# One-hot weights of the second token block shared out three ways, and 24 retrieved rows added during that stage

## The reference, cut to what matters

```
expert, gate = product-key top-k(h)            # 128 experts for each token
act = gelu(einsum('td,ted->te', h, u_table[expert]))
out = einsum('te,ted->td', gate * act, v_table[expert])
x = LayerNorm(alpha * x + (1 + gate2) * out) * ln2_g + ln2_b
```

## Time and profile before

| what | value |
| --- | --- |
| median of 3 runs | 2711.09 us (2710.27 to 2713.92) |
| the profiled execution | 2719.48 us |
| its span | 2717.0 us |
| PE busy | 2374.5 us, 87% |
| DVE busy | 2061.6 us, 76% |
| ACT busy | 1009.8 us, 37% |
| POOL busy | 869.9 us, 32% |

### The profile page before, as it was taken

One profiled execution on the slowest core, in us unless ns is written; L12 is line 12 of the kernel. 1 busy time (PEld: TensorE's weight loads), 2 busy tenths in 40 slices (PEclk: granted clock), 3 DMA queues, 4 the chain that ended last, 5 costly groups with the idle time before them and its releaser, 6 DMA issues.

```text
span 2717.0 us, 34317 instructions
## 1 busy us (share of the span) xinstructions
PE 2374.5 (87%) x12532; PEld 1891.1 (70%) x12532; DVE 2061.6 (76%) x2517; ACT 1009.8 (37%) x1428; POOL 869.9 (32%) x733
## 2 busy tenths in 40 slices
PE   4799999999999999999969867666666699999996
PEld 3688877888888887888859857656656664444442
DVE  7777779788888786554576999999999786665577
ACT  2254543344444444433343322227776750000000
POOL 0000011222222221000001566656666454444344
PEclk9799999999999999999989988887787799999998
DMA  9767669566666565555746899999999879999997
GB/s 385 292 215 243 226 228 358 208 213 215 217 217 215 207 215 193 207 189 186 258 178 230 353 419 419 419 419 388 404 407 388 344 256 414 413 413 414 414 413 277
DMA packets 144867, 819.86 MB, mean 302 GB/s; under 512 B 16680, under 2 KB 19360, under 8 KB 70480
## 3 DMA queue, kind: packets, MB, share of 16 engines
q0 software_dynamic: 93200, 477.21, 44.7%
q1 hardware_dynamic: 48480, 335.95, 33.3%
q10 hardware_dynamic: 3040, 4.68, 0.5%
HBM read 813.55 MB, written 4.23 MB: 301 GB/s over the span
## 4 chain that ended last, share of the span: by engine, by line
PE 61%; DVE 23%; DMA 7%; issue 5%; ACT 3%; POOL 1%; ACTq 0%; DVEq 0%; POOLq 0%
PE aux L1155 16%; DVE rrow L2151 9%; PE ps L706 8%; PE ps L707 8%; PE ps L712 7%; PE ps L731 4%; PE ps L732 4%; PE ps L737 4%; DMA rrow<-in_peer_u,acc 3%; DVE acc L1668 2%; DVE rrow_first L2151 1%; DVE wlo L1619 1%; PE aux L992 1%; DMA dskip<-in_D_skip 1%; DMA vden<-in_p_vd 1%
## 5 line engine op out<-in xcount | busy, mean ns | idle before, releaser
L1619 DVE TENSOR_TENSOR wlo<-raw,whi 128x2048 fp32r<-128x2048 f32 x216 | 499.6, 2314 | 292.4 <-ACT whi L1174 281.8
L1174 ACT ACTIVATE whi<-raw 128x2048 fp32r<-128x2048 f32 x216 | 412.1, 1910 | 664.1 <-PE ps L712 386.8
L2236 DVE SCALAR_TENSOR_TENSOR ps<-vrow,acc,ps 128x1024 f32<-128x1024 f32 x231 | 297.5, 1288 | 177.2 <-DMA vrow<-in_p_vg,acc 162.1
L2414 POOL DMA_INDIRECT rrow<-in_peer_u,acc x219 | 354.1, 1617 | 220.3 <-DVE dots L2151 115.2
L2151 DVE CUSTOM_DVE_ANT_0 rrow<-rrow,h 128x2048 f32<-128x2048 f32 x172 | 385.1, 2288 | 16.8 <-DMA rrow<-in_peer_u,acc 16.3
L2414 POOL DMA_INDIRECT vrow<-in_p_vg,acc x256 | 247.4, 966 | 265.3 <-DVE ps L2236 178.0
L2328 POOL DMA_DIRECT2D ada_in<-in_p_ada x128 | 69.3, 542 | 673.2 <-DVEq L1775 529.2
L1096 PE MATMUL aux<-hT,rT 128*128 128x128 f32 x1792 | 233.8, 294 | 37.1 <-ACT rT L1503 37.1
L731 PE MATMUL ps<-h_hi,whi 128*128 128x256 f32 x1040 | 264.6, 295 | 0.0
L1096 PEld LDWEIGHTS aux<-hT,rT 128*128 128x128 f32 x1792 | 226.7, 209 | 46.0 <-issue 31.7
L706 PE MATMUL ps<-whi,h_hi 128*128 128x512 f32 x576 | 235.1, 408 | 24.7 <-ACT whi L1174 24.1
(11 more groups left out here) (361 smaller groups left out, 4337.7 us busy)
## 6 DMA issues: line engine op xcount, KB each, us to landing
raw<-in_p_in SPq DMA_DIRECT2D x104, 1024.0 KB, 4.9
ada_in<-in_p_ada POOLq DMA_DIRECT2D x128, 512.0 KB, 4.8
vden<-in_p_vd SPq DMA_DIRECT2D x64, 1024.0 KB, 8.0
ada_in<-in_p_ada SPq DMA_DIRECT2D x32, 1024.0 KB, 10.1
raw<-in_p_so SPq DMA_DIRECT2D x32, 1024.0 KB, 4.7
raw<-in_p_mo SPq DMA_DIRECT2D x16, 1024.0 KB, 7.2
raw<-in_p_bc SPq DMA_DIRECT2D x16, 1024.0 KB, 6.4
raw<-in_p_mix SPq DMA_DIRECT2D x16, 1024.0 KB, 4.8
```

Source lines behind the costliest of these rows:

```text
L1174: F(whi[:, n % 2, :, 0:cols_], raw[:, n % 4, :, 0:cols_], ACT.Copy).then_inc(hi_ready, 1)
L1619: V.tensor_tensor(wlo[:, n % 2, :, 0:cols_], raw[:, n % 4, :, 0:cols_], whi[:, n % 2, :, 0:cols_].bitcast(F32), ALU.subtract).then_inc(lo_ ...
L2236: last = V.scalar_tensor_tensor(o, row, w, o, ALU.mult, ALU.add)
L2414: return G.indirect_dma_start(out=dst, out_offset=None, in_=table, in_offset=bass.IndirectOffsetOnAxis(ap=eid_all[:, r:r + 1], axis=0))
```

## The change

The three kinds of groups are laid out in a pattern of eight: three WEIGHED (as before: VectorE compares both tiles, ScalarE multiplies), four ALL_DVE (VectorE compares the first tile, and makes the second in four fused compare-and-multiply instructions of 128 columns) and one ALL_ACT (ScalarE makes both by squares, then 1 - x clipped at zero, then the multiplication, as the first block's groups are made; the squares are issued one and two groups ahead). In the weights stage 24 rows are added instead of 8: TensorE adds the even rows 0 to 22, after groups 1, 4 and 7 of each eight, and VectorE the odd rows 1 to 23, after groups 0, 3 and 6, into the idle bank pair 1. After the stage VectorE copies pair 1 to SBUF and adds it to pair 0, and only then may SP load `vden` units 2 and 3 (the copy lies in their memory). VectorE then goes on from row 24 instead of row 8. The diff, cut:

```
+        def made(n):
+            return (WEIGHED, ALL_DVE, WEIGHED, ALL_DVE, ALL_DVE, ALL_ACT, WEIGHED, ALL_DVE)[n % 8]
...
-        FIRST_PE, TAIL_PE = OHB // 4, range(225, BLK * SEL, 2)
+        FIRST, TAIL_PE = 24, range(225, BLK * SEL, 2)
+        FIRST_PE = range(0, FIRST, 2)
...
                         sp_.wait_ge(wt_done, BLK * OHB)
+                        sp_.wait_ge(merged, merged_before + 1)
...
                     weights_of(1, n)
-                    if n % 4 == 3:
-                        pe_add(n // 4, n // 4 == 0, n // 4 == FIRST_PE - 1)
+                    if n % 8 in (1, 4, 7):
+                        r = FIRST_PE[n // 8 * 3 + (1, 4, 7).index(n % 8)]
+                        pe_add(r, r == FIRST_PE[0], r == FIRST_PE[-1])
...
+                def squares(n, half):
+                    act.wait_ge(wt_done, OHB + n - 3)
+                    for t in range(2 * half, 2 * half + 2):
+                        for k in range(2):
+                            last = F(oh[1][:, n % 4, k, t, :], niota, ACT.Square, scale=-1.0,
+                                     bias=selT[:, k, n * OHT + t:n * OHT + t + 1])
...
+                def hots(n):
...
+                    F(flat, flat, ACT.Relu, scale=-1.0, bias=con[:, C_ONE:C_ONE + 1]).then_inc(act_step, 1)
+                    act.wait_ge(act_step, done)
...
                 for n in range(OHB):
-                    if by_act(n):
+                    for half in range(2):
+                        if n + 2 - half < OHB and made(n + 2 - half) == ALL_ACT:
+                            squares(n + 2 - half, half)
+                    if made(n) == ALL_ACT:
+                        hots(n)
+                    if made(n) != ALL_DVE:
                         weigh(n)
...
-                    o = ps[:, r // SEL, :, :].rearrange("p a n -> p (a n)")
+                    o = ps[:, 1 if r < FIRST else r // SEL, :, :].rearrange("p a n -> p (a n)")
...
+                    elif made(n) == ALL_DVE:
+                        V.tensor_tensor(o[:, 0], niota.unsqueeze(1).broadcast_to([P, OHT, P]),
+                                        selT[:, 0, t4].unsqueeze(2).broadcast_to([P, OHT, P]), ALU.is_equal)
+                        for t in range(OHT):
+                            token = n * OHT + t
+                            last = V.tensor_scalar(o[:, 1, t, :], niota, selT[:, 1, token:token + 1],
+                                                   selT[:, 2, token:token + 1], ALU.is_equal, ALU.mult)
+                        last.then_inc(oh_ready, 1)
+                    if n % 8 in (0, 3, 6):
+                        add_row(2 * (n // 8 * 3 + n % 8 // 3) + 1)
+                dve.wait_ge(vrow_pe_used, scores_all + len(FIRST_PE))
+                dve.wait_ge(vrow_used, adds_by(False, FIRST - 1))
+                dve.wait_ge(wt_done, BLK * OHB)
+                both = [ps[:, k, :, :].rearrange("p a n -> p (a n)") for k in range(2)]
+                link(V.tensor_copy(on_dve[:, :], both[1]))
+                link(V.tensor_tensor(both[0], both[0], on_dve[:, :], ALU.add))
+                dve.sem_inc(merged, 1)
...
-                for r in range(FIRST_PE, BLK * SEL):
+                for r in range(FIRST, BLK * SEL):
...
-                    if r < FIRST_PE:
+                    if r in FIRST_PE:
                         weight_diagonal(r)
```

More of the change, by code:

```diff
@@ L327, in build, with steps_made @@
         oh = [at(f"oh{b}", o * KB, [P, OHN[b], 2, OHT, P]) for b, o in enumerate((150, 62))]
[L329 to L335, removed]
+        WEIGHED, ALL_DVE, ALL_ACT = range(3)
+        def made(n):
+            return (WEIGHED, ALL_DVE, WEIGHED, ALL_DVE, ALL_DVE, ALL_ACT, WEIGHED, ALL_DVE)[n % 8]
+        def steps_made(kinds, n):
+            return sum(made(k) in kinds for k in range(n + 1))
         QA = KEYS // 2
@@ L360, in build @@
         DV, NVU = D // 2, KEYS // 2
+        on_dve = at("on_dve", 62 * KB, [P, DV])
         vrow = at("vrow", 14 * KB, [P, ROWS, D - DV])
@@ L370, in build @@
         vden = at("vden", 46 * KB, [P, 4, 2, DV])
-        FIRST_PE, TAIL_PE = OHB // 4, range(225, BLK * SEL, 2)
-        adds_on_pe = list(range(FIRST_PE)) + list(TAIL_PE)
+        FIRST, TAIL_PE = 24, range(225, BLK * SEL, 2)
+        FIRST_PE = range(0, FIRST, 2)
+        adds_on_pe = list(FIRST_PE) + list(TAIL_PE)
         late = BLK * SEL - 64
@@ L542, in build @@
         block0_read, block0_before = c_ready, 1
+        act_step, act_before = sumsq_ready, 4
+        merged, merged_before = neg_a, 1
         held = sem("held")
@@ L1108, in weights_of @@
                     m, k = b * OHB + n, n % OHN[b]
-                    if b and by_act(n):
-                        pe.wait_ge(hot_done, OHB + steps_by(True, n))
+                    if b and made(n) != ALL_DVE:
+                        pe.wait_ge(hot_done, OHB + steps_made((WEIGHED, ALL_ACT), n))
                     else:
-                        pe.wait_ge(oh_ready, OHB + steps_by(False, n) if b else n + 1)
+                        pe.wait_ge(oh_ready, OHB + steps_made((ALL_DVE,), n) if b else n + 1)
                     before = m - OHN[b] if n >= OHN[b] else OHB - 1 if b else -1
@@ L1524, in weights_out @@
                     last.then_inc(wt_read, 1)
+                def squares(n, half):
[4 more added lines that the diff above has]
+                                     bias=selT[:, k, n * OHT + t:n * OHT + t + 1])
+                    if half:
+                        last.then_inc(act_step, 1)
+                def hots(n):
+                    done = act_before + 2 * steps_made((ALL_ACT,), n)
+                    act.wait_ge(act_step, done - 1)
+                    flat = oh[1][:, n % 4].rearrange("p k t i -> p (k t i)")
+                    F(flat, flat, ACT.Relu, scale=-1.0, bias=con[:, C_ONE:C_ONE + 1]).then_inc(act_step, 1)
+                    act.wait_ge(act_step, done)
                 def weigh(n):
-                    act.wait_ge(square_done, OHB + steps_by(True, n))
+                    if made(n) == WEIGHED:
+                        act.wait_ge(square_done, OHB + steps_made((WEIGHED,), n))
                     for t in range(OHT):
@@ L1597, in tail_diagonal @@
                     n = adds_by(True, r) - 1
-                    act.wait_ge(vrow_pe_used, scores_all + max(FIRST_PE, n - 3))
+                    act.wait_ge(vrow_pe_used, scores_all + max(len(FIRST_PE), n - 3))
                     F(diag[n % 4], ident, ACT.Copy, scale=w_all[:, r:r + 1]).then_inc(diag_ready, 1)
@@ L2224, in add_row @@
                 def add_row(r):
-                    o = ps[:, r // SEL, :, :].rearrange("p a n -> p (a n)")
+                    o = ps[:, 1 if r < FIRST else r // SEL, :, :].rearrange("p a n -> p (a n)")
                     row, w = vrow[:, vrow_slot(r), :], w_all[:, r:r + 1]
                     dve.wait_ge(vrow_full[r % ROWS], vrow_before[r % ROWS] + 16 * (r // ROWS + 1))
-                    if r % SEL == 0:
+                    if r in (1, SEL):
                         last = V.tensor_scalar(o, row, w, None, ALU.mult)
                     else:
[L2232 to L2235, removed]
+                        dve.wait_ge(vrow_used, adds_by(False, r - 1))
                         last = V.scalar_tensor_tensor(o, row, w, o, ALU.mult, ALU.add)
@@ L2243, in _ @@
                 for n in range(OHB):
-                    if n >= 4:
-                        dve.wait_ge(wt_done, OHB + n - 3)
                     o = oh[1][:, n % 4]
                     t4 = slice(n * OHT, n * OHT + OHT)
[L2248 to L2255, removed]
+                    if n >= 4 and made(n) != ALL_ACT:
+                        dve.wait_ge(wt_done, OHB + n - 3)
@@ new lines, in _ @@
+                    if made(n) == WEIGHED:
+                        V.tensor_tensor(o, niota.unsqueeze(1).unsqueeze(1).broadcast_to([P, 2, OHT, P]),
+                                        selT[:, 0:2, t4].unsqueeze(3).broadcast_to([P, 2, OHT, P]), ALU.is_equal)\
+                            .then_inc(square_done, 1)
+                    elif made(n) == ALL_DVE:
[6 more added lines that the diff above has]
+                        last.then_inc(oh_ready, 1)
```

## The result

The changed kernel took 2722.88 us (median of 13 runs, 2718.07 to 2728.29), the kernel before, run with it, 2715.82 (13 runs). The ratio is 1.0029, with a 95% interval of 1.0020 to 1.0037: 7.9 us slower (the two medians alone differ by 7.1). On the median that the forecast started from, that is 2719.0, against 2720.8.

The account below looks back on a forecast made before the run. TensorE's own matmul pace was taken as the bound: start of the dense stage + 447.5 + 56.4 us. Weights stage +9.7, merge, dense stage and tail 0, sum +9.7 on 2711.09: 2720.8 us, range 2707 to 2729.

Parts of the forecast that it names:

- Weights stage, +9.7: Stage before the dense matmuls: grows from 49.4 to 59.1 us, VectorE's sum 52.1; bounds +2.3 to +17.
- The high end of my bounds: Spacing of a fused instruction on VectorE in the weights stage: 0.15 to 0.283 us, 0.2 taken.
- Entry, exit and coupling: Weights stage beyond VectorE's sum: 5.0 us entry and exit, plus 2 us (0 to 4) for waits between engines.
- GpSimd and the rows at nothing: Weights stage: four more diagonals and 16 more gathers on GpSimd cost nothing, as it works up to eight rows ahead.
- the first rival: Weights stage: supply of rows binds, dense stage starts at 2230, +17 us, 2728; chance 0.12.
- Merge at nothing: Between weights and dense stages: VectorE's 2.6 us merge and the later load of units 2 and 3 cost 0 (0 to 6).
- The second rival: Start of dense stage: units 2 and 3 come late behind the merge, +9.7 and up to 6 us, 2727; chance 0.06.
- Dense stage at nothing: Dense stage: 8.4 MB fewer to gather gains TensorE 0, at most the whole 8.0 us.
- GpSimd's wait of some 39 us: End of dense stage: row 232 issued some 32 us earlier, GpSimd waiting some 39 us instead of 6.88 for row 225.
- Tail unchanged: After the dense stage: the wait for row 225 and the 23 gathers behind it stay the same, 0.
- The last two rivals: Dense stage: relief returns 8.0 us where DMA holds TensorE (0.17); DMA sets dense stage and tail, 2700.5 (0.10).
- the third rival: Dense stage: relief pays where DMA holds TensorE, 8.0 us come back, 2713, or 2706 at the stage's floor; chance 0.17.

Follow-up runs that it names:

- after_tail: Changed kernel with TensorE's share of the last rows beginning at row 241 instead of 225; 0.9975 of the kernel before.
- rows_only: Changed kernel with the old split of groups, keeping the 24 rows and the merge; 1.0046 of the kernel before, +12.5 us.
- before_tail: Kernel before with TensorE's share of the last rows beginning at row 241 instead of 225; 0.9996, not told from no change.
- fused_only: Kernel before with the fused form in VectorE's own eleven groups only; single execution, time not compared, weights stage 48.8 us.
- skip64: Kernel before with the gathers of rows 16 to 79 (33.6 MB) replaced by tiny loads; 0.9992, not told from no change.
- skip16: Kernel before with the gathers of rows 16 to 31 (8.4 MB) replaced by tiny loads; 0.9991, not told from no change.
- split_only: Changed kernel with the three-way split of groups but only the old eight rows, all on TensorE; 1.0032 of the kernel before, +8.7 us.

## Why the prediction was right, and where it was not

The path was right: the time is TensorE's string, and its +8.1 us are the +9.9 of the weights stage, less 2.7 in the dense stage, plus 0.9 in the tail. That 2719.0 came so near to 2720.8 is partly luck, since two errors cancel inside the +9.9, and the other two parts had been put at nothing.

**Weights stage, +9.7: +9.9.** Right in sum, with two errors that cancel. VectorE has 54.9 us of work without a gap, not 52.1: the 64 fused instructions take 17.3 us (54.9 less 12 compares at 1.14, 16 at 0.60 and 12 additions at 1.19), 0.27 each where I took 0.2; that is +4.5, and additions and compares at their spacing give 1.7 back. The high end of my bounds, 0.283, was near. Entry, exit and coupling came to 59.25 - 54.9 = 4.3, not 5.0 + 2: with VectorE plainly the bound, no coupling shows. In the split alone, where ScalarE binds, it does.

**GpSimd and the rows at nothing: right.** Gathers took 1343 ns on average in the groups above, against 937 in the dense stage. The Trainium skill (GPSIMD Engine Reference, Key points) says that GpSimd shares its SBUF interfaces with VectorE and contends with its instructions that have two SBUF inputs or run in a two-port mode. The two means agree with that, but no run here isolates this cause. In the kernel before's stage its eleven gathers took 1495 ns on average, so the change didn't make them slower; no addition waited for a gather, and the first rival falls.

**Merge at nothing: right.** It ends at 2220.31, and the first 672 dense matmuls run through in 288.41 us, the same as before. The second rival falls.

**Dense stage at nothing: -2.7.** The stall is shorter in after than in before. TensorE's timeline of after:

```profile
2529.99 3.29 PE L1163 MATMUL aux<-vden,wt0b 128*128 128x512 f32 x4 [3.21 <-DMA vden<-in_p_vd]
2533.08 2.31 PE L1163 MATMUL aux<-vden,wt 128*128 128x512 f32 x4
2535.23 1.02 PE L1163 MATMUL aux<-vden,wt0b 128*128 128x512 f32 x2
```

And of before:

```profile
2526.86 3.78 PE L1155 MATMUL aux<-vden,wt0b 128*128 128x512 f32 x4 [4.59 <-DMA vden<-in_p_vd]
2530.44 3.11 PE L1155 MATMUL aux<-vden,wt 128*128 128x512 f32 x4
2533.39 1.88 PE L1155 MATMUL aux<-vden,wt0b 128*128 128x512 f32 x4
```

Of the 2.7, 1.4 are the wait and 1.3 the eight matmuls behind it (5.24 us to the next start after, 6.53 before, 3.44 undisturbed). It isn't the relief by itself: with 8.4 or 33.6 MB less and the old weights stage the dense stage took 447.0 and 447.2. The wait goes with the added rows and their merge: 3.2 to 3.4 us in after, after_tail and rows_only (dense stage 444.6 to 444.7), 4.5 to 4.7 in the six kernels without them that keep the stall. Of those six, before_tail and fused_only have a dense stage of 445.9 and 445.8 by losing less behind the wait. Why it is shorter with them stays open. TensorE stalls 309 us into the stage, not 282 as I wrote, which is where the 5 MB are issued; nothing hung on that.

**GpSimd's wait of some 39 us: 20.5.** This step failed in size. I took 16 rows at 2.03 us, the mean over the whole stage, and the rows at its two ends are not at the mean. GpSimd's timeline at rows 31 and 224 of before, then of after (rows 15 and 232 of before stand in the earlier trace rows):

```profile
2239.09 0.94 POOL L2414 DMA_INDIRECT vrow<-in_p_vg,acc  x1 [0.46 <-issue]
2644.16 0.94 POOL L2414 DMA_INDIRECT vrow<-in_p_vg,acc  x1 [0.66 <-issue]
```

```profile
2219.84 0.94 POOL L2457 DMA_INDIRECT vrow<-in_p_vg,acc  x1 [0.30 <-issue]
2626.88 0.94 POOL L2457 DMA_INDIRECT vrow<-in_p_vg,acc  x1 [0.46 <-issue]
```

Before, rows 15 to 31 took 25.0 us, 1.56 each, so at row 31 the lead against the start of the dense stage is 23.8 us (26.0 less 2.2), not 32. At row 224 it is 21.8. The last eight rows take 11.1 us before, 1.39 each, and 16.6 after, and so take 5.5 more of it. Row 232 was issued 425.9 us into the dense stage, before 442.2: 16.3 us earlier, of which the shorter dense stage takes 2.7 and the rest is the added wait (20.51 - 6.88 = 13.6). Bytes over the full rate, 20.3 us, stood in the same paragraph and was nearer. Since the wait was idle time either way (41.3 us of it in skip64 didn't change the time), the total didn't suffer.

**Tail unchanged: +0.9.** Row 233 is gathered 2.7 us after the end of the dense stage in both. In skip16, skip64 and split_only, whose tails nothing touched, the tail took 56.3 to 56.7, and in rows_only, with the added rows, 56.5. The chain shows where the 0.9 lies, in the landing of row 254 (before, then after), behind which both kernels take 17.1 us to the end:

```profile
2693.06 6.85 DMA vrow<-in_p_vg,acc
2694.66 8.03 DMA vrow<-in_p_vg,acc
```

That is 1.2 us more for one gather, which was issued 0.2 earlier after the dense stage. One trace of each doesn't tell whether that belongs to the change; in rows_only it is 7.2.

**The last two rivals** (the relief pays in the dense stage; DMA sets everything) fall with skip64: its window shows TensorE's pace unchanged, and its stall is as long as in the kernel before. The 2.7 us that did come back are less than the 8.0 of the third rival, and the relief in bytes alone doesn't give them. The relief went into GpSimd's wait for row 225.

## What to carry to other kernels

When work is moved out of a stage with full DMA, ask first which engine's string sets that stage's length, and follow the lead that the other string gains to the place where it is stopped; here that was one buffer that the late engine frees. A lead is worth nothing until that stop is moved, and moving the stop alone is worth nothing until the lead is there: the change alone made the kernel 0.29% slower, the moved stop alone 0.04% faster, which isn't told from nothing, and both together made it 0.25% faster. (With the norm's loads spread out as well and the stop at row 233 it is 0.06 and 0.29%.) Saturated DMA beside a fully busy TensorE doesn't tell which of them leads; taking bytes away does.

## What the runs showed of the hardware that was not expected

- The compare-and-multiply with two scalars from memory, on 128 fp32 columns, lasts 341 to 367 ns on average (split_only, after) and stands at a spacing of 0.26 to 0.27 us, dearer than the 228 ns of the tensor-scalar in the earlier trace rows.
- A stall of TensorE cost more than its length: 4.59 us of waiting were followed by eight matmuls that took 3.1 us more than undisturbed ones. A window of the kernel before shows the granted clock at half behind the stall, the lower of the two levels, 1.2 of 2.4 GHz:

```profile
2500.00:2520.00 20.00, 20.00 (x48) 8.80 (x47) 7.13 (x6) 0.00 (x0) 5.62 (x6) 1.00 1.02 416
...
2527.00:2532.00 5.00, 5.00 (x6) 2.05 (x7) 1.32 (x2) 0.00 (x0) 1.35 (x2) 0.50 1.02 418
```
- With five loads of 1 MB issued together ahead of the next table, TensorE waited 4.6 us for it; with the same loads spread over nine units it waited for none (dense stage 447.3 against 439.5 us).
